# FFN down projections of two of three parts as pairs of output blocks, half of their depth by seven products

## The reference, cut to what matters

```python
def swiglu(x, w_gu, w_d):                      # w_gu (1024, 5632), w_d (2816, 1024)
    a, b = jnp.split(x @ w_gu, 2, axis=-1)
    return (jax.nn.silu(a) * b) @ w_d

for i in range(2):
    x = x + 0.5 * swiglu(rmsnorm(x, norm_g[i, 0]), ffn_w_gu[i, 0], ffn_w_d[i, 0])
    x = x + mixer_i(rmsnorm(x, norm_g[i, 1]))  # DeltaNet and mLSTM heads (i=0), gated convolution (i=1)
    x = x + 0.5 * swiglu(rmsnorm(x, norm_g[i, 2]), ffn_w_gu[i, 1], ffn_w_d[i, 1])
    x = x + (p[i] @ w_ple[i]) * jax.nn.sigmoid(rmsnorm(x, norm_g[i, 3]) @ w_ple_gate[i])
```

## Time and profile before

| | |
|---|---|
| median of 3 runs | 2701.01 us (2698.94 to 2701.26) |
| profiled execution: span | 2701.0 us, 43738 instructions; no other time of that execution is given |
| PE busy | 2659.5 us (98%), 18234 matmuls |
| PE weight load busy | 2619.8 us |
| DVE busy | 1863.6 us (69%) |
| ACT busy | 1070.8 us (40%) |
| POOL busy | 529.8 us (20%) |
| DMA | 205.57 MB, mean 76 GB/s |
| mean granted TensorE clock | 0.994 of full speed |

### The profile page before, as it was taken

The page is one execution under the profiler, slowest core; times in us unless marked ns, Lnnn a source line. Parts: engine busy times, 40 slices in busy tenths (PEclk is TensorE's granted clock), DMA queues, the critical chain, the costliest instruction groups (busy, mean ns, idle before and its releaser), DMA issues.

```text
span 2701.0 us, 43738 instructions
## 1 busy us (share of the span) xinstructions
PE 2659.5 (98%) x18234; PEld 2619.8 (97%) x18234; DVE 1863.6 (69%) x2179; ACT 1070.8 (40%) x1559; POOL 529.8 (20%) x251
## 2 busy tenths in 40 slices
PE   9999999999999999999999999999999999999998
PEld 9999999999999799999999999999999999999998
DVE  7748386987677678476577974848666786574756
ACT  5425253243223545344345552524411254252545
POOL 2130303332010030302113302030333311102041
PEclk9999999999999799999999999999999999999999
DMA  4223223232003122223232232232222223232231
GB/s 133 84 72 85 79 75 90 57 79 55 17 9 87 56 86 79 79 79 94 63 90 69 82 91 71 80 92 75 85 79 77 63 79 94 63 97 66 81 103 49
DMA packets 401148, 205.57 MB, mean 76 GB/s; under 512 B 15554, under 2 KB 398939, under 8 KB 400952
## 3 DMA queue, kind: packets, MB, share of 16 engines
q1 hardware_dynamic: 400746, 202.70, 26.4%
q10 hardware_dynamic: 206, 0.08, 0.0%
HBM read 195.14 MB, written 7.60 MB: 75 GB/s over the span
## 4 chain that ended last, share of the span: by engine, by line
PE 81%; DVE 15%; ACT 2%; issue 1%; DMA 0%; POOL 0%; DVEq 0%; SPq 0%; ACTq 0%
PE ps L913 12%; PE ps L917 12%; PE ps L928 12%; PE ps L914 12%; PE ps L930 12%; PE ps L929 12%; PE ps L1062 3%; PE ps L1088 2%; DVE ut L2207 1%; DVE x L2941 1%; DVE ct L2996 1%; DVE r L2392 1%; DVE ct L2993 1%; DVE sumsq L2306 1%; PE ps L1056 1%
## 5 line engine op out<-in xcount | busy, mean ns | idle before, releaser
L861 POOL TENSOR_TENSOR wlo<-raw,whi 128x1024 fp32r<-128x1024 f32 (+2 forms) x214 | 518.3, 2425 | 2131.9 <-ACT whi L1637 2131.7
L913 PE MATMUL ps<-xh,whi 128*128 128x320 f32 x1552 | 472.3, 312 | 8.0 <-POOL wlo L861 5.8
L914 PE MATMUL ps<-xl,whi 128*128 128x320 f32 x1552 | 467.0, 309 | 0.0
L913 PE MATMUL ps<-hh,whi 128*128 128x320 f32 x1440 | 436.3, 311 | 4.1 <-POOL wlo L861 1.9
L914 PE MATMUL ps<-hl,whi 128*128 128x320 f32 x1440 | 433.6, 309 | 0.0
L928 PE MATMUL ps<-tau_hi,whi 128*128 128x320 f32 x1280 | 396.4, 310 | 2.9 <-DVE wlo L2223 2.0
L929 PE MATMUL ps<-tau_lo,whi 128*128 128x320 f32 x1280 | 395.5, 309 | 0.0
L930 PE MATMUL ps<-tau_hi,wlo 128*128 128x320 f32 x1280 | 395.5, 309 | 0.0
L1637 ACT CAST whi<-raw 128x1024 fp32r<-128x1024 f32 (+2 forms) x216 | 208.5, 967 | 390.8 <-PE ps L917 352.0
L917 PE MATMUL ps<-xh,wlo 128*128 128x320 f32 x1552 | 353.4, 309 | 0.0
L917 PE MATMUL ps<-hh,wlo 128*128 128x320 f32 x1440 | 328.1, 309 | 0.0
(11 more groups left out here) (435 smaller groups left out, 4827.5 us busy)
## 6 DMA issues: line engine op xcount, KB each, us to landing
raw<-in_ffn_w_gu SPq DMA_DIRECT2D x320, 256.0 KB, 3.8
raw<-in_ffn_w_d SPq DMA_DIRECT2D x64, 512.0 KB, 4.0
raw<-in_w_in_even SPq DMA_DIRECT2D x32, 512.0 KB, 4.1
raw<-in_ffn_w_d SPq DMA_DIRECT2D x32, 384.0 KB, 3.6
raw<-in_w_in_odd SPq DMA_DIRECT2D x24, 512.0 KB, 3.7
raw<-in_ffn_w_gu SPq DMA_DIRECT2D x16, 512.0 KB, 4.2
raw<-in_w_ple_gate SPq DMA_DIRECT2D x16, 512.0 KB, 3.8
raw<-in_w_out_even SPq DMA_DIRECT2D x8, 512.0 KB, 4.4
```

Source lines behind the costliest of these rows:

```text
L861: pool.tensor_tensor(ring(wlo, n), raw[:, slot, 0:kt, :], ring(whi, n).bitcast(fp32), ALU.subtract).then_inc(lo_ready, 1)
L913: pe.matmul(ps[j % 4][:, c, 0:HT], wh[:, k], hi[:, k, cs], start=(k == 0), stop=False)
L914: pe.matmul(ps[j % 4][:, c, 0:HT], wh[:, k], lo[:, k, cs], start=False, stop=False)
```

## The change

Parts 0 and 1 of each FFN get a new down stage. Output blocks are taken in pairs, 4 per stage. Of the 8 hidden tiles, 0, 1, 4 and 5 go through the seven products (2 tiles per product), and 2, 3, 6 and 7 are multiplied plainly into the same four banks. The third part keeps the plain down stage.

What follows from it:
- `mm_down` on TensorE. In the first pair of a stage the plain tiles come last, tiles 2, 3, 6 and then 7; in the three others they stand between the fifth and the sixth product.
- A fifth group of weights (the plain tiles, slots 3 to 6, upper halves) beside the four of a pair; ring slots are tracked by halves.
- All low parts of these weights are made by VectorE; GpSimd made those of the down blocks.
- Sums of hidden tiles 0, 1, 4, 5 (`tau_rows`, `taus_high`, `taus_low`) are made during the gate/up stage, on VectorE and ScalarE.
- Per pair two sums with copies (`down_sums`) and two updates of x (`down_x`) on VectorE. Those of the last pair stand in the next gate/up stage.
- 8 DMAs of 128 KB per pair, for 2 of 512 KB.
- A memset of R1 moves from GpSimd to VectorE, and GpSimd makes its level masks before block 8 instead of block 12.

```diff
+        def mm_down(p, s, first):
...
+            product(b1, 0, xs(high, 0, 0), xs(low, 0, 0), True, kt=DM)
+            wait_slot(jy)
+            product(b2, 1, xs(high, 1, 0), xs(low, 1, 0), True, kt=DM)
+            pe.wait_ge(pair_copied, 4 * p + 1)
+            pe.wait_ge(pair_lo, group_at(p, 1))
+            if first:
+                pe.wait_ge(h_tau_low, s["tau0"] + 2)
+            product(b1, 2, ts(0, 0), ts(1, 0), False, kt=DM)
+            product(b3, 3, ts(0, 1), ts(1, 1), True, kt=DM)
+            pe.wait_ge(pair_copied, 4 * p + 2)
+            product(b1, 4, ts(0, 2), ts(1, 2), False, kt=DM)
+            if first:
+                pe.wait_ge(pair_lo, group_at(p, 2))
+                product(b4, 5, ts(0, 3), ts(1, 3), True, kt=DM)
+                pe.wait_ge(pair_copied, 4 * p + 3)
+                pe.wait_ge(pair_lo, group_at(p, 3))
+                product(b3, 6, xs(high, 1, 1), xs(low, 1, 1), False, kt=DM, signal=False)
+                pe.wait_ge(pair_lo, group_at(p, 4))
+                pe.wait_ge(pair_copied, 4 * p + 4)
+                for ks in ((2, 3, 6), (7,)):
+                    pe.wait_ge(h_ready, s["hbase"] + ks[-1] + 1)
+                    for out, col, half in ((b2, 0, 0), (b4, 1, 0), (b3, 0, 1), (b1, 1, 1)):
+                        last = plain(out, col, half, ks)
+                last.then_inc(prod_done, 1)
+            else:
+                pe.wait_ge(pair_lo, group_at(p, 4))
+                plain(b2, 0, 0, (2, 3, 6, 7))
+                plain(b4, 1, 0, (2, 3, 6, 7), start=True)
+                pe.wait_ge(pair_copied, 4 * p + 3)
+                plain(b3, 0, 1, (2, 3, 6, 7))
+                pe.wait_ge(pair_copied, 4 * p + 4)
+                plain(b1, 1, 1, (2, 3, 6, 7))
+                pe.wait_ge(pair_lo, group_at(p, 2))
+                product(b4, 5, ts(0, 3), ts(1, 3), False, kt=DM)
+                pe.wait_ge(pair_lo, group_at(p, 3))
+                product(b3, 6, xs(high, 1, 1), xs(low, 1, 1), False, kt=DM)
...
+                    last_use[c, e] = ("pair", 7 * n + ((6 if pair_src[n][1] else 7) if down and e else ORDER.index(c) + 1))
...
+                    for q, (half, c) in enumerate(((1, col + P), (0, col + P), (0, col), (1, col))):
+                        sp.dma_start(quarter(p, q)[:, 0:DM], rows[0, half][:, :, c:c + P]).then_inc(raw_loaded[raw_pos["pair", p]], 16)
...
+                    def tau_rows(q):
...
+                        if q % 4 == 0:
+                            o1(dve.tensor_tensor(row[1], hf[:, 0:HT], hf[:, HT:T], ALU.subtract))
+                            return
+                        o1(dve.tensor_tensor(row[0], hf[:, HT:T], row[1], ALU.subtract))
+                        dve.wait_ge(h_kept, s["tau0"] + i + 1)
+                        o1(dve.scalar_tensor_tensor(row[2], hf[:, HT:T], -1.0, row[2], ALU.mult, ALU.subtract))
+                        own(dve.tensor_tensor(row[3], hf[:, 0:HT], row[0], ALU.subtract).then_inc(h_tau_rows, 1), h_tau_rows)
...
+                    def down_sums(p):
...
+                        dve.tensor_tensor(halves(gt[:]), P2(jy), halves(first_copy[:]), ALU.add).then_inc(slot_free[jy % 4], 1)
+                        dve.tensor_tensor(halves(ut[:]), P2(jx), halves(second_copy[:]), ALU.add).then_inc(slot_free[jx % 4], 1)
...
                     else:
+                        for d in range(KD // 2):
+                            p = s["d0"] + d
...
+                            down_sums(p - 1)
+                            pair_low(p, 4)
+                            pair_low(p, 2)
+                            pair_low(p, 3)
+                            first = sums_13(p + 1)
+                            down_x(p - 1, 2 * d - 2, 0)
+                            sums_2(p + 1, first)
+                            pair_low(p + 1, 0)
+                            down_x(p - 1, 2 * d - 1, 1)
+                            sums_4(p + 1)
+                            pair_low(p + 1, 1)
```

More of the change, by code:

```diff
@@ L77, in stream_step @@
         KH = KD // 2
+        DM = KH // 2
         NS = 7
@@ L385, in pair_blk, with is_down, pair_copies, copies_user @@
             return len(pair_src) - 1
+        group0 = []
+        def is_down(p):
+            return pair_src[p][2] is not None
+        def pair_copies(p):
+            if is_down(p) and pair_src[p][1] // (2 * P) % 2:
+                return stt, hf
+            return pcopy, qcopy
+        def copies_user(p):
+            same = [m for m in range(max(0, p - 2), p) if pair_copies(m)[0] is pair_copies(p)[0]]
+            return same[-1] if same else None
+        def groups(p):
+            return 5 if is_down(p) else 4
+        def group_at(p, g):
+            if is_down(p) and pair_src[p][1]:
+                return group0[p] + [0, 1, 3, 4, 2][g] + 1
+            return group0[p] + g + 1
         stages = []
@@ L433, in ffn_stage @@
                 last = part == len(PARTS) - 1
+                s["taus"], s["after"], s["d0"], s["hid"], s["hbase"] = not last, part > 0, len(pair_src), other(prod - 1), first_pair + j0
+                if not last:
+                    s["tau0"] = rounds
+                    rounds += 2
+                    for o in range(0, KD, 2):
+                        pair_blk(dn, o * P, j0 * P)
+                    j0 += cnt
+                    continue
                 s = dict(kind="down", n0=len(blocks), kt=cnt, last=last, scale=-0.5, hbase=first_pair + j0, layer=i, tau=None, hid=other(prod - 1),
@@ L613, in stream_step @@
                 hi_user[kind, n, g] = [(k, max(v for k_, v in uses if k_ == k)) for k in sorted({k for k, _ in uses})]
[L614 to L615 removed]
+                for c, e in group:
+                    if kind == "block":
+                        last_use[c, e] = ("block", done_at(block_job[n]))
+                    else:
+                        last_use[c, e] = ("pair", 7 * n + ((6 if pair_src[n][1] else 7) if down and e else ORDER.index(c) + 1))
             turn += len(spots)
@@ L691, in load_pair @@
             def load_pair(p):
-                w, col = pair_src[p]
+                w, col, row = pair_src[p]
+                if row is not None:
+                    rows = w[row:row + KD * P].rearrange("(k two e p) c -> two e p k c", two=2, e=2, p=P)
+                    free_spot("pair", p)
+                    for q, (half, c) in enumerate(((1, col + P), (0, col + P), (0, col), (1, col))):
+                        sp.dma_start(quarter(p, q)[:, 0:DM], rows[0, half][:, :, c:c + P]).then_inc(raw_loaded[raw_pos["pair", p]], 16)
+                    for q in range(4):
+                        a, c = (row + (4 * (q % 2) + 2) * P), col + q // 2 * P
+                        sp.dma_start(quarter(p, q)[:, DM:KH], w[a:a + DM * P, c:c + P].rearrange("(k p) c -> p k c", p=P)).then_inc(raw_loaded[raw_pos["pair", p]], 16)
+                    return
                 rows = w.rearrange("(k two p) c -> two p k c", two=2, p=P)
@@ L733, in _ @@
                             load(n, source(n))
-                    for p in range(s["p0"], s["p0"] + s["count"] - s["plain"]):
+                    for p in range(s["p0"], s["p0"] + s["count"] - s["plain"] + (KD // 2 if s["taus"] else 0)):
                         load_pair(p)
@@ L831, in _ @@
             pool.sem_inc(ident_ready, 1)
-            step(pool.memset(R1[:], 0.0))
             step(pool.memset(incl[:], 1.0))
@@ L919, in mm, with product @@
                     last.then_inc(job_done, 1)
-            def product(out, slot, hi, lo, start, ready=None):
-                for i in range(KH):
+            def product(out, slot, hi, lo, start, ready=None, kt=KH, signal=True):
+                for i in range(kt):
                     if ready is not None:
@@ L2919, in _ @@
                             hidden(q - 1)
+                            tau_rows(q - 1)
+                        elif not q and s["after"]:
+                            down_x(p - 1, KD - 2, 0)
                         if more:
```

275 lines of the change are left out of this document (221 added, 54 removed).

## The result

The changed kernel takes **2668.0 us** (median of 4 runs, 2664.95 to 2669.65) against 2701.1 for the kernel before on the same chip (4 runs, 2698.94 to 2702.36): ratio 0.9876, 95% interval 0.9864 to 0.9888, or 33.1 us faster. 2667 was forecast, 2662 to 2684. The profiled span is 2664.9 us; that execution took 2666.6.

The account below looks back on a forecast made before the run. TensorE, busy 98% of the span, was taken as the bound. The terms were summed as 2701.0 - 28.2 - 4.6 - 3.9 + 1.0 + 1.9 + 0.2 = 2666.4 us, rounded up to 2667; range 2662 to 2684.

Parts of the forecast that it names:

- 192 matmuls at 0.1467 us: Eight down stages: 6 fewer matmuls in each of 4 pairs per stage, 28.2 us less.
- The start wait: Start of each down stage: TensorE's 0.58 us wait for tile 7's low part goes, 4.6 us less.
- The end wait: Behind each down stage: the 0.49 us wait for the next pair's weight low parts goes, 3.9 us less.
- The copies: Down pairs: ACT's partial-product copies end just early enough to be free; 1.0 us added for jitter.
- DVE in a down pair: DVE takes over POOL's low parts: 10.1 us of work in a 13.2 us pair, hidden, nothing added.
- The opening: Opening of the first FFN: new DVE operations for activation sums lengthen TensorE's wait at 79.63, 1.9 us more.
- A: Rival: only the matmuls go, the 8.5 us of stage waits stay, moved elsewhere: 2675; chance 0.22, together with D.
- B: Rival: ACT's copies in down pairs come too late, 0.31 us for each of 64: 2686; chance 0.12.
- C: Rival: DVE becomes the bound of the down pairs, a pair taking 15.2 us: 2730; chance 0.04.
- D: Rival: opening costs double or the reordered ring adds a 0.5 us stall per stage: 2672; chance 0.22, together with A.
- The +0.2 us for the second layer's first FFN: Second layer's first FFN, with two plain tiles: activation sums there add 0.2 us.
- Transfers and POOL at zero: Smaller DMAs have time, and the DVE memset and POOL's earlier level masks lie beside idle time: zero.

Follow-up runs that it names:

- tile7_late: Kernel before the change, with hidden tile 7 of block 0 multiplied after two tiles of block 1 in the 8-tile parts too: 2695.23 us, ratio 0.9986.
- copies_13: Changed kernel with ScalarE's two early partial-product copies of each down pair (1 and 3) made twice: 2693.77 us.
- low_twice: Changed kernel with the low part of the plain group's weights made twice on DVE in each down pair: 2673.41 us.
- levels_late: Changed kernel with GpSimd's level masks made one block later, outside the opening: 2668.37 us, ratio 0.9886.
- no_first: Changed kernel with the plain down stage kept in the first part of the first FFN, so seven stages changed: 2672.26 us, ratio 0.9893.
- copies_45: Control: changed kernel with ScalarE's two later partial-product copies of each down pair (4 and 5) made twice: 2667.16 us.

## Why the prediction was right, step by step

1. **192 matmuls at 0.1467 us, 28.2 us.** Right: 18042 matmuls, and 52.80 us for 360 of them.
2. **The start wait, 4.6 us.** Right. tile7_late had 3.8 for it alone, and 4.6 by its trace. One number in the working was wrong: `late` is false for parts of 8 tiles, so tile 7 was wanted after 42 matmuls and not 54, 6.2 us after the last pair and not 7.9. 125.46 + 6.16 = 131.62 is just where the wait in the earlier trace rows begins. The term is read from the wait, so the sum didn't change.
3. **The end wait, 3.9 us.** Right, ready at 2.64 where 2.7 was worked out, and the gate/up stage behind has no wait.
4. **The copies, 1.0 us for jitter.** Right that they are free, and the term should have been 0: no stage has a gap. copies_13 shows how near: 0.42 us more costs 0.77 a pair. The rule of the Trainium skill (ScalarE: Activation LUTs, Rules for kernel authors) that the prediction held against this, an estimated 0.57 us, is stated for an ACTIVATE with a pointer operand as bias. These are plain copies without one, and they take 0.43 in the earlier trace rows and here.
5. **DVE in a down pair.** Right, 9.5 us in place of 10.1, since the update of x takes 0.83 where POOL does not work, not 1.10. low_twice found the margin (0.4 us in pair 2) that the sum gave: deadline 4.4, ready at 3.8, and 0.16 before the slot to be free.
6. **The opening, 1.9 us.** This is the term that was mis-sized: it cost 4.8. (Of the rivals, A, B and C did not happen; D's "the opening costs double" did.) The new operations were counted almost right, 1.8 us on DVE by the trace where 1.95 was worked out, but they were not all. DVE began the gate of tile 3 at 78.00 in place of 74.78, 3.2 us later, and 3.5 after the FFN's beginning, which came 0.25 us earlier in this execution (tau_lo at 45.93 for 46.18). The masks on POOL lengthened DVE's operations between 68 and 77 us by 0.7; levels_late gave back 0.6 (77.37). The last part is POOL's low part, which the new order meets at other operations. After:

```profile
57.80 2.49 POOL L956 TENSOR_TENSOR wlo<-raw,whi 128x1024 fp32r<-128x1024 f32 x1 [12.59 <-ACT whi L1801]
```

and before, on DVE:

```profile
59.55 1.95 DVE L2820 TENSOR_TENSOR hl<-hf,hh 128x640 fp32r<-128x640 f32 x1
61.54 2.42 DVE L2261 TENSOR_SCALAR xg_back<-x,vec 128x320 f32<-128x320 f32 x1
```

Before, these two took 1.95 and 2.42 us where their kinds take 0.83 and 0.39: 3.15 lost. After, one of 0.49 and one of 0.55 took 2.59 and 2.57: 4.12 lost, 1.0 more. The Trainium skill (SBUF — State Buffer, SBUF: two separate sides) says that a VectorE operation in a 2-port mode, or one with two SBUF inputs beside a GpSimd operation that reads SBUF, and the GpSimd operation take turns, each holding the other off for its whole length. The trace agrees: the DVE operation at 58.05, with two SBUF inputs, began while POOL's ran and ended 0.35 us behind it. So 1.8 + 0.7 + 1.0 = 3.5, which is what DVE's rows show. TensorE's first product on sums started 3.2 us later with it (82.84 against 79.63); the stop at 76.00 costs nothing by itself, since the later one would have been longer by it. The clock added 1.5. Both together are 4.7 of the 4.8 us.

In the earlier trace rows I had followed the low part, and passed over the copy that ends 0.4 us before it and that the last row names. The copy's chain runs through the same gate of tile 3 and its silu.

The +0.2 us for the second layer's first FFN did not come: its wait fell from 0.53 us (at 1544.59) to 0.32 (at 1527.70).

7. **Transfers and POOL at zero.** Right for the stages: no wait names a DMA. Wrong for the masks: "beside idle time" was true of POOL and not of DVE, whose operations in the opening lengthened (1.49 to 1.72 at 70.00); levels_late won 0.6 us in the opening by moving them and lost it again at 413 us.

**The total** is wrong in its addition: the terms as written make 2667.4, not 2666.4. The stated 2667 hides it. With the terms as they turned out, the sum is 2701.1 - 28.2 - 8.5 + 4.8 - 0.2 = 2669.0, 1.0 above the median measured, and the runs vary by more (2664.95 to 2669.65). So the mechanism of the stages was right to a tenth of a microsecond, and that the total met 2668.0 within 1 us was in part luck: the opening was 2.9 too cheap, and against it stood 1.0 for copies that cost nothing, 0.4 for the second layer, and what the runs vary by. The prediction set the span of the profiled execution of before equal to the median time. In every later execution the time is 1.7 us above the span, so that one took an estimated 2702.7, 1.7 above its median; the sum starts from 2701.0, the median, and is not changed by it. The rival with the dearest side, C, was priced by slow DVE operations; they went with POOL's work.

What stays open: how the opening's loss divides between the masks and the new operations. DVE's rows add up, but the parts are not independent: by DVE's gate the masks are worth 0.6 us in levels_late, and 1.1 in no_first, where the gate began at 75.90 without any new operation. No run puts the masks back where they were before while the rest of the opening is repaired.

## What to carry to other kernels

Where a stage's work stands beside slack, the matmul count times the measured start-to-start step is the gain, and each hidden term is a deadline to be checked against a clock time, since busy shares (72% on DVE here, 0.4 us from a stall) say nothing of it. Openings and other one-time stretches are where a change to many equal stages loses what the sum didn't see: there follow every engine's queue back from the waiting instruction, as two chains may end at the same wait, and shortening one shows nothing. A repair is to be looked at in the whole trace, since work moved out of one stretch can come late in another.

## What the runs showed of the hardware

- The clock after a stop: in this opening, after waits of 2.99, 3.09 (3.09 and 3.10 in three more executions) and 4.05 us PE went to the lower level for 3 to 6 us (granted clock 0.53 and 0.57 in such a stretch); after 0.61, 1.15 and 2.11 us it stayed at 1.00. Between 2.11 and 2.99 nothing was measured. So shortening a wait from 3.1 to 1.15 gave back 3.4 us, not 1.9. The price is not fixed: the changed kernel lost 1.5 us by it, copies_45 some 2.6 after a stop of the same length, with 20 slow steps for 13. Nor is a long stop the only cause: in every execution the clock fell in the mixer between 865 and 945 us too, where no stop is over 0.9 us.
- A late matmul costs a little more than its lateness: the next step is 0.07 to 0.11 longer (132.43 to 132.68, 76.00 to 76.22).
- POOL's mask operations, of 128 x 128 elements, stretched DVE's by up to 15% (1.49 to 1.72), and were stretched themselves: one alone takes 0.29 us, two beside DVE's took 2.11 (at 69.98). POOL's 1024-element low part held a DVE operation of 0.5 us for 2.6.
